# Seven-product matrix groups of a three-block transformer kernel: partial products chained in three PSUM pairs and added straight into the output quadrants

## The reference

```python
def sq_relu_mlp(h, w_up, w_down):          # twice: layers 0 and 1, D_FF = 4096
    return jnp.square(jax.nn.relu(h @ w_up)) @ w_down
...
    u = causal_depthwise_conv(h @ w_up[l].astype(h.dtype), ffn_conv_w[l], ffn_conv_b[l])
    u_val, u_gate = jnp.split(u, 2, axis=-1)   # width D_FF_2 = 2816 each
    x = x + (jax.nn.silu(u_gate) * u_val) @ w_down[l].astype(x.dtype)
```

## Time and profile before

| | |
|---|---|
| median of 3 runs | 1903.86 us (1903.72 to 1904.85) |
| span of the profiled execution | 1900.5 us |
| matmuls / DVE / ACT instructions | 9486 / 1988 / 1587 |
| DVE and ACT busy | 1339.4 and 985.3 us |

### The profile page before, as it was taken

How to read it: one execution, slowest core, us unless ns; L and a number is a source line. 1 busy time by engine, 2 the same in 40 slices (tenths; PEclk the granted TensorE clock), 3 DMA queues, 4 the chain that set the end, 5 groups by cost and what they waited for, 6 DMA issues and landing times. The chain is left out here.

```text
span 1900.5 us, 25399 instructions
## 1 busy us (share of the span) xinstructions
PE 1890.5 (99%) x9486; PEld 1555.8 (82%) x9486; DVE 1339.4 (70%) x1988; ACT 985.3 (52%) x1587; POOL 95.3 (5%) x114
## 2 busy tenths in 40 slices
PE   9999999999999999999999999999999999999999
PEld 8877888887888778888888988667788888888887
DVE  7656665656566766665566788998897867767867
ACT  5634464544546746454444435788445446545454
POOL 0100000101000000000100000000000000100101
PEclk9999999999999999999999999999999999999999
DMA  7632156757323114756752356222224634644735
GB/s 230 155 100 94 73 142 180 166 162 202 123 79 144 46 56 132 201 139 173 180 162 67 112 143 167 89 90 78 89 91 143 166 89 155 155 148 118 199 95 122
DMA packets 69676, 249.79 MB, mean 131 GB/s; under 512 B 7730, under 2 KB 7986, under 8 KB 68916
## 3 DMA queue, kind: packets, MB, share of 16 engines
q1 hardware_dynamic: 55728, 198.88, 31.0%
q0 software_dynamic: 13824, 49.29, 14.8%
q10 hardware_dynamic: 4, 0.00, 0.0%
HBM read 246.05 MB, written 2.10 MB: 131 GB/s over the span
## 5 line engine op out<-in xcount | busy, mean ns | idle before, releaser
L545 PE MATMUL ps<-HH,WH 128*128 128x512 f32 (+1 forms) x1696 | 626.2, 369 | 0.9 <-ACT AT L1736 0.9
L547 PE MATMUL ps<-HH,WL 128*128 128x512 f32 (+1 forms) x1696 | 621.2, 366 | 0.0
L546 PE MATMUL ps<-HL,WH 128*128 128x512 f32 (+1 forms) x1696 | 620.9, 366 | 0.0
L1299 ACT ACTIVATE WH<-WR 128x1024 fp32r<-128x1024 f32 x333 | 348.9, 1056 | 479.8 <-PE ps L547 315.3
L2030 DVE TENSOR_TENSOR WL<-WR,WH 128x1024 fp32r<-128x1024 f32 (+1 forms) x332 | 403.1, 1218 | 263.1 <-ACT WH L1299 262.4
L545 PEld LDWEIGHTS ps<-HH,WH 128*128 128x128 f32 x1696 | 319.9, 189 | 62.5 <-issue 11.6
L547 PEld LDWEIGHTS ps<-HH,WL 128*128 128x128 f32 x1696 | 319.9, 189 | 52.2
L546 PEld LDWEIGHTS ps<-HL,WH 128*128 128x128 f32 x1696 | 320.0, 189 | 50.7
L959 PE MATMUL ps<-WH,AH 128*128 128x512 f32 x490 | 191.0, 390 | 0.4 <-DVE WL L2030 0.4
L960 PE MATMUL ps<-WH,AL 128*128 128x512 f32 x490 | 190.7, 389 | 0.0
L961 PE MATMUL ps<-WL,AH 128*128 128x512 f32 x490 | 190.6, 389 | 0.0
(11 more groups left out here) (386 smaller groups left out, 2606.9 us busy)
## 6 DMA issues: line engine op xcount, KB each, us to landing
WR<-in_up SPq DMA_DIRECT2D x96, 512.0 KB, 4.2
WR<-in_quart SPq DMA_DIRECT2D x60, 512.0 KB, 3.6
WR<-in_quart POOLq DMA_DIRECT2D x48, 512.0 KB, 6.3
WR<-in_in SPq DMA_DIRECT2D x48, 512.0 KB, 3.6
WR<-in_down SPq DMA_DIRECT2D x16, 512.0 KB, 3.5
WR<-in_quartf SPq DMA_DIRECT2D x14, 512.0 KB, 3.5
WR<-in_quartf POOLq DMA_DIRECT2D x14, 512.0 KB, 5.6
MT<-in_up SPq DMA_DIRECT2D x12, 512.0 KB, 4.1
```

Of the source, the lines that this page charges most:

```text
L545: e.matmul(ps, wh, hi[:, c, cols], start=c == 0, stop=False)
L546: e.matmul(ps, wh, lo[:, c, cols], start=False, stop=False)
L547: y = e.matmul(ps, wl, hi[:, c, cols], start=False, stop=c == x.n - 1)
L1299: e.activation(x.wh[:, 0:n], raw(m, x.raw)[:, 0:n], AF.Copy).then_inc(*k.mark("whi", u))
```

## The change

The order of a group becomes b11, b21, t1 (half 0), b11, b21, t1 (half 1), then t2, b22, t3, t4. Seven products now use three pairs of banks: t2 goes on adding in the pair of b11, t3 goes on in that same pair, b22 goes on in the pair of t1, and t4 starts afresh in the pair of b21. Each time the pair has been taken out once before the next product continues in it, and PE waits for that. With the running sums, each `part` goes straight to the output quadrants: seven products make eight DVE operations a group, one each and two for t3. The accumulators PX and U2 and the `together` operations go. The first write to a quadrant is a copy, or a multiplication by -1 for t2. The groups of sevenf0 and sevenf1 do the same on X, and their POOL adds now go by `M_SUMS`. In `seven`, DVE now does the `part` that is due ahead of the cut of unit j+3. The last four down units wait for the last unit of the third group instead of `together`. Fewer matmuls start with an overwriting write; their number and shapes stay.

```diff
@@ -225,7 +225,7 @@
         add(f"up{layer}3", up[24:])
-        add(f"down{layer}3", down, extra=m.EXTRA["mlp"], freed=("sum7", layer, 6))
+        add(f"down{layer}3", down, extra=m.EXTRA["mlp"], freed=("unit", at[f"seven{layer}2"] + 13))
         if layer == 0:
@@ -315,13 +315,11 @@
     m.AL = arena("AL", [128, 4, 7, 256], 28, F32R)
-    m.PX = arena("PX", [128, 3, 2, 512], 59)
     m.H3H = arena("H3H", [128, DC, T], 0, F32R)
...
     m.SF = arena("SF", [128, 2, 4, 256], 56)
-    m.U2 = arena("U2", [128, 2, 512], 64)
@@ -385,13 +383,6 @@
-def partial(m, what):
-
-    if what in ("b21", "t2", "t3"):
-        return m.PX[:, ("b21", "t2", "t3").index(what)]
-    return quarter(m, *{"b11": (0, 0), "b22": (0, 1), "t4": (1, 0), "t1": (1, 1)}[what])
-
-
 def mixes(m, key):
@@ -473,7 +464,7 @@
 GLA_O = (6, 7)
-STREAM = [("b11", 0), ("b21", 0), ("t1", 0), ("b11", 1), ("b21", 1), ("t1", 1), ("b22", 0), ("b22", 1), ("t2", 0), ("t2", 1),
+STREAM = [("b11", 0), ("b21", 0), ("t1", 0), ("b11", 1), ("b21", 1), ("t1", 1), ("t2", 0), ("t2", 1), ("b22", 0), ("b22", 1),
           ("t3", 0), ("t3", 1), ("t4", 0), ("t4", 1)]
@@ -481,7 +472,7 @@
 M_SUMS = [("t1", 0), ("t1", 1), ("t2", 0), ("t2", 1), ("t3", 0), ("t3", 1), ("t4", 0), ("t4", 1)]
-F_SUMS = [("t1", 0), ("t1", 1), ("t2", 0), ("t3", 0), ("t3", 1), ("t2", 1), ("t4", 0), ("t4", 1)]
+LAST_SUMS = [("t1", 0), ("t1", 1), ("t2", 0), ("t3", 0), ("t3", 1), ("t2", 1), ("t4", 0), ("t4", 1)]
 LAST_BANKS = {"b11": 0, "b21": 2, "t1": 4, "b22": 6, "t2": 0, "t3": 0, "t4": 2}
@@ -495,9 +486,10 @@
 V_DECAYS, V_TURNS = (1, 4, 7, 10), (3, 6, 9, 12)
-SEVEN_BANKS = {"b11": 0, "b21": 2, "t1": 4, "b22": 6, "t2": 0, "t3": 2, "t4": 4}
-FFN_PARTS = {"b11": (((0, 0), 1), ("u2", 1)), "b21": (((0, 0), 1),), "t1": (((0, 1), 1), ((1, 1), 1)), "b22": (((0, 1), 1),),
-             "t2": (("u2", 1),), "t3": (((1, 0), 1), ((1, 1), -1)), "t4": (((1, 0), 1),)}
+SEVEN_BANKS = {"b11": 0, "b21": 2, "t1": 4, "b22": 4, "t2": 0, "t3": 0, "t4": 2}
+SEVEN_STARTS = ("b11", "b21", "t1", "t4")
+SEVEN_PARTS = {"b11": (((0, 0), 1),), "b21": (((0, 0), 1),), "t1": (((1, 1), 1),), "t2": (((0, 1), -1),), "b22": (((0, 1), 1),),
+               "t3": (((1, 1), -1), ((1, 0), 1)), "t4": (((1, 0), 1),)}
 GLA_DS = ((2, 3), (4, 5))
@@ -956,9 +948,9 @@
             e.wait_ge(*k.on("side", key, 4 * o + p, SIDE_PART[f]))
-            e.matmul(m.ps[b + v], xh, x.wh[:, w], start=start and q == 0, stop=False, skip_group_check=last)
-            e.matmul(m.ps[b + v], xl, x.wh[:, w], start=False, stop=False, skip_group_check=last)
-            y = e.matmul(m.ps[b + v], xh, x.wl[:, w], start=False, stop=stop and q == n - 1, skip_group_check=last)
+            e.matmul(m.ps[b + v], xh, x.wh[:, w], start=start and q == 0, stop=False, skip_group_check=True)
+            e.matmul(m.ps[b + v], xl, x.wh[:, w], start=False, stop=False, skip_group_check=True)
+            y = e.matmul(m.ps[b + v], xh, x.wl[:, w], start=False, stop=stop and q == n - 1, skip_group_check=True)
         return y
@@ -976,7 +968,7 @@
                 e.wait_ge(*k.on(*k.free[b + v]))
-            y = pairs(j, h, b, f, v, h == 0 and not (last and what in ("t2", "t3")), h == 1)
+            y = pairs(j, h, b, f, v, h == 0 and what in SEVEN_STARTS + ("b22",) * last, h == 1)
             if last and what == "t2" and h and v == 0:
@@ -2426,6 +2418,7 @@
     post, then = ("post_mlp0", "mix1") if layer == 0 else ("post_mlp1", "in2")
+    prior = {}
@@ -2442,22 +2435,27 @@
         u = at[f"seven{layer}{o}"] + STREAM.index((what, 1))
-        src, acc = pair(m, SEVEN_BANKS[what]).rearrange("p (a f) -> p a f", a=2), partial(m, what)
+        src = pair(m, SEVEN_BANKS[what]).rearrange("p (a f) -> p a f", a=2)
         e.wait_ge(*k.on("unit", u))
-        if o == 0:
-            e.tensor_copy(acc, src).then_inc(*k.mark("part", layer, o, what))
-        else:
-            e.wait_ge(*k.on("part", layer, o - 1, what))
-            e.tensor_tensor(acc, src, acc, A.add).then_inc(*k.mark("part", layer, o, what))
-
-    def together(n):
-
-        c11, c12, c21, c22 = (quarter(m, i, j) for i in range(2) for j in range(2))
-        p2, u2, u3 = (m.PX[:, i] for i in range(3))
-        out, a, b, op = ((u2, c11, u2, A.add), (c11, c11, p2, A.add), (u3, u2, u3, A.add), (c21, c21, u3, A.add),
-                         (c12, c12, c22, A.add), (c12, c12, u2, A.subtract), (c22, c22, u3, A.subtract))[n]
-        e.wait_ge(*(k.on("sum7", layer, n - 1) if n else k.on("part", layer, 2, "t4")))
-        e.tensor_tensor(out, a, b, op).then_inc(*k.mark("sum7", layer, n))
+        for to, sign in SEVEN_PARTS[what]:
+            acc = quarter(m, *to)
+            if to not in prior:
+                if layer == 0:
+                    e.wait_ge(*k.on("turned", "mlp0", 3, 1))
+                else:
+                    e.wait_ge(*k.on("turned", "mlp1", 3, 1))
+                if sign > 0:
+                    e.tensor_copy(acc, src).then_inc(*k.mark("part", layer, o, what, to))
+                else:
+                    e.tensor_scalar(acc, src, -1.0, None, A.mult).then_inc(*k.mark("part", layer, o, what, to))
+            else:
+                e.wait_ge(*k.on("part", *prior[to]))
+                if sign > 0:
+                    e.tensor_tensor(acc, src, acc, A.add).then_inc(*k.mark("part", layer, o, what, to))
+                else:
+                    e.tensor_tensor(acc, acc, src, A.subtract).then_inc(*k.mark("part", layer, o, what, to))
+            prior[to] = (layer, o, what, to)
+        k.also("part", layer, o, what)
@@ -2467,7 +2465,6 @@
                     plain(24 + j - 1)
-                    together(j - 1)
                 continue
@@ -2480,13 +2477,13 @@
         for j in range(14):
+            if j and STREAM[j - 1][1]:
+                part(o, STREAM[j - 1][0])
             v_cut(e, k, u + j + 3)
...
                 v_side_s(e, k, layer, 4 * o + 3)
-            if j and STREAM[j - 1][1]:
-                part(o, STREAM[j - 1][0])
         part(o, STREAM[13][0])
@@ -2896,8 +2893,6 @@
             v_cut(e, k, f_unit(k, j) + 4)
-            if a == 32 and n in (1, 3, 5):
-                together(n // 2)
             if n > 1 and n % 2 == 0:
@@ -2919,13 +2914,11 @@
             e.wait_ge(*k.on("unit", u))
-        for to, sign in (LAST_PARTS if o == 2 else FFN_PARTS)[what]:
-            acc = (m.U2[:, :, :] if to == "u2" else quarter_x(*to))[:, vs]
+        for to, sign in (LAST_PARTS if o == 2 else SEVEN_PARTS)[what]:
+            acc = quarter_x(*to)[:, vs]
             if to in prior:
                 e.wait_ge(*k.on("part", "f", *prior[to]))
-            if to == "u2" and not o and what == "b11":
-                e.tensor_copy(acc, src).then_inc(*k.mark("part", "f", o, what, to))
-            elif sign > 0:
+            if sign > 0:
                 e.tensor_tensor(acc, src, acc, A.add).then_inc(*k.mark("part", "f", o, what, to))
@@ -2934,19 +2927,14 @@
-    def together(n):
-
-        acc, op = ((quarter_x(0, 1), A.subtract), (quarter_x(1, 0), A.add), (quarter_x(1, 1), A.subtract))[n]
-        e.wait_ge(*k.on("part", "f", 1, "t4"))
-        e.tensor_tensor(acc, acc, m.U2[:, :, :], op).then_inc(*k.mark("part", "f", "u2", n))
-        prior[((0, 1), (1, 0), (1, 1))[n]] = ("u2", n)
-
     def seven(o):
...
                 break
+            if j and o < 2 and stream[j - 1][1]:
+                part(o, stream[j - 1][0])
             v_cut(e, k, u + j + 3)
@@ -2954,8 +2942,6 @@
                 v_side_s(e, k, "f", LAST_HIDDEN[o] // 2)
-            if j and o < 2 and stream[j - 1][1]:
-                part(o, stream[j - 1][0])
         if o < 2:
@@ -3013,7 +2999,7 @@
     u = k.at[name]
-    for what in F_SUMS if key == "f" else M_SUMS:
+    for what in LAST_SUMS if name == "sevenf2" else M_SUMS:
         j = stream_of(name).index(what)
```

## The result

The changed kernel takes 1953.35 us (median of 5, 1950.76 to 1954.81) beside 1903.72 us: the ratio is 1.0259, with a 95% interval of 1.0247 to 1.0271. It is slower by about 50 us. The forecast was 1937 with a range up to 1950: the direction and the place of the loss were right, the size was too small, and the range ended 3 us too low.

A forecast was written before the change was run, and what follows sets the result against it. PE, 99% busy, was taken as the bound. Waits of 17.6 us (four quiet groups), 14.1 (two with gain loads) and 1.3 (sevenf0, sevenf1) sum to 33.0 on 1900.5, plus 3.4 around the span: 1936.9 us; range 1914 to 1950.

The forecast's parts named there:

- DVE's saving: Fifteen fewer DVE operations at 1.22 us: 18 us off DVE, 0 off the end, since PE doesn't wait for them.
- The chain: Weight sums: b22 and t3 share a raw slot, so PE waits at unit 10, 4.4 us in each quiet group.
- Step 2: In seven00, unit 8's cut on DVE waits behind unit 7's cut and b21's part: begins at 287.7, done at 288.9 us.
- Step 3: In seven00, t3's load follows unit 8's cut, so t3's add goes out at 292.6 us, 6.3 us later.
- Step 4: In seven00, t2's part stands behind unit 10's cut and ends at 301.9; unit 10 is due at 297.5: 4.4 us wait.
- sevenf0 and sevenf1: Gated layer's two groups: t1's part slightly late for unit 8, 0.6 us each, 1.3 in all; bounds 0 and 3 each.
- the rival of the falling clock: Clock falls to 1.2 GHz for one unit after each of six waits, 2.7 us each: 1953 us; chance 0.09.
- a wait of 7.7 us each: In seven02 and seven12, t2's add takes 8.8 us beside the gain tile; 14.1 us together, less seven02's 1.3 of today.
- The section on the PSUM pairs: Continuing pairs have two units, 5.4 us, for a 1.22 us part: fits t2 and b22 in quiet groups; t3 depends on DVE.
- The prediction's own signs: Right: eleventh unit late, t3's add at 22 us, groups 42 to 46 us, DVE near 1321 us. Wrong: clock at 0.5.
- the rival with quicker transfers: Adds in the chain take 4.4 us once they run apart, so groups wait less: 1917 us; chance 0.14.
- PE's pace in the groups: Faster rival: without accumulator traffic the 0.227 us between matmuls falls; 11 ns less gains 14.8 us: 1889 us; chance 0.03.

The follow-up runs named there:

- e8_both: Changed kernel with own raw slots for t3, t1's half 1 earlier, t2's part ahead of unit 10's cut, bank ring from 4, later gain tiles: 1902.94 us, ratio 0.9993.
- e1_slots: Changed kernel with two raw slots of their own for t3's halves in the six groups of layers 0 and 1: 1910.02 us, ratio 1.0031.
- e6_order_dve: Kernel before with the new order of products and DVE's new order, but accumulators and four PSUM pairs kept (no chaining): 1940.81 us, ratio 1.0196.
- e2_warm: Changed kernel with 16 matmuls whose result nobody reads ahead of unit 10 in the six groups of layers 0 and 1: 1939.92 us, ratio 1.0189.
- e3_part: Changed kernel with DVE doing t2's part ahead of unit 10's cut in the six groups of layers 0 and 1: 1943.12 us, ratio 1.0205.
- e4_order: Kernel before with only t2 ahead of b22 in the groups' order and M_SUMS for sevenf0 and sevenf1: 1949.6 us, ratio 1.0242.
- e7_gain: Changed kernel with the two 1 MB gain tiles loaded only behind the up units after the third groups: 1945.64 us, ratio 1.0220.

## Why the prediction was right and wrong

**DVE's saving is hidden: right.** DVE's busy time fell by 16 us, the sum said 18, and e8_both shows that it is worth nothing measurable at the end (0.9984 to 1.0002).

**The chain: right step by step in seven00, and in sum with some luck.** t2's second add went out 8.4 us after the group's first matmul, as before. It took 5.3 us where I took 5.5:

```profile
DMA to landing us min/median/max: 5.3/5.3/5.3
```

Step 2 put unit 8's cut 17.3 us into the group, and it began at 288.16 - 271.09 = 17.1. Step 3 put t3's add at 22.2 us, and it went out at 293.26 - 271.09 = 22.2. Step 4 gave PE's restart at 31.5 us and it was 31.2; the stop was 4.0 us, not 4.4. The other three groups without a gain tile stopped for 4.8, 6.5 and 4.4 us, the two with one for 7.3 and 6.8, where I had 7.7. Together, less the 1.3 us of before, that is 32.4 us against the forecast's 31.7. The closeness is in part luck: the quiet groups stopped for 19.6 us where I had 17.6, and the other two added 12.8 where I had 14.1. e1_slots shows by removal that the shared slot is the cause, and e6_order_dve shows the same wait when the order is added without the chaining.

**sevenf0 and sevenf1: right.** 1.0 us together, against 1.3. The steps of the prediction gave a wait of 0.4 us each (1661.1 less 1660.7), and it took 0.6 without saying why; the stops were 0.3 and 0.5 us.

**What failed.** The step is the one that let each wait cost its own length: "a wait of 7.7 us each" and "4.4 us in each", summed with PE at full pace behind them. I had this as the rival of the falling clock, priced at 16 us, and gave it 0.09, because no row of before showed a stop that long. It happened in all six groups and cost 13.2 us. e2_warm, which fills the stops with work, gets 13.4 us back by the medians. With it the sum is 1950, and a wait that I overlooked adds 1.6: the twelve last up units begin at bank 2, which is now t4's, and its part is not done when sevenf1 ends. The section on the PSUM pairs looked at the groups alone and put nothing down for this:

```profile
1848.76 0.39 PE L953 MATMUL ps<-WL,AH 128*128 128x512 f32 x1
1850.55 0.47 PE L537 MATMUL ps<-HH,WH 128*128 128x512 f32 x1 [1.41 <-DVE X L2922]
```

That makes 1952, and 1953.35 was measured (1951.54 in the profiled execution). The 3.4 us that the prediction set around the span came from two different executions, and in each one on record it is 1.8 to 2.5 us; the sum adds to the median, so nothing hangs on it. The bounds had the same gap: I let the clock rival fall outside the range as one case in ten, though by the forecast itself stops of 4 to 8 us were the likely case, and the only question was what the clock does behind one. The prediction's own signs came out mixed: the late eleventh unit, t3's add 22 us into the group and DVE at 1323 us spoke for it, the granted clock at its lower level against it, and the groups lasted 43.8 to 48.1 us where it had 42 to 46.

**The other rivals.** The adds did not come down to the 4.4 us of the rival with quicker transfers: in the four groups without a gain tile t2's second add took 5.3 to 5.6 us and t3's 5.4 to 7.8. By the Trainium skill, page "DMA: Bandwidth & Descriptors", section "Anatomy of one DMA", the estimate was 3.2 us; the trace doesn't agree. PE's pace in the groups didn't change: 0.227 us from start to start wherever the clock is at its upper level.

## What to carry to other kernels

Where one engine is busy for 99% and waits for nobody, work taken from another is worth nothing, and an order that leaves a chain of slots and transfers less time can only cost: write down, for each unit that moves, which buffer its load takes and who must be done with it. When an operation has to stand in an engine's queue, put it ahead of what waits for a transfer, if its own input is ready first. And when a new wait of several microseconds is forecast on PE, price the clock behind it along with the wait.

## What the runs showed of the hardware

In the groups of seven of the changed kernel, e3_part, e4_order, e6_order_dve and e7_gain PE stopped for 2.3 us or more thirty times. Behind 29 of these stops the granted clock went to its lower level, for 6 to 14 matmuls of 128x512, which took 0.427 us from start to start instead of 0.227; the shortest such stop was 2.3 us. In five cases the first two to four matmuls behind the stop still ran at full pace. Behind one stop, of 3.35 us (e3_part, seven01), and behind all of up to 2.1 us the clock stayed up, so the length of a stop alone does not settle it. The Trainium skill, page "TensorE: Matmul & The Clock Gate", section "HAM oscillation", says that PE's idle stretches while it waits for a DMA bring the lower clock, and here the trace agrees in all but that one. In the changed kernel a stop of 4 to 6.7 us cost another 1.6 to 2.8 us. With sixteen matmuls whose result nobody reads ahead of the wait, the clock stayed up in five groups of six, in one of them behind 3.0 us of stop that were left, and the kernel took 13.4 us less.

An adding DMA of 512 KB (t2's second one in a group) took 5.3 to 5.6 us nearly alone in the changed kernel, 6.9 to 8.1 us when t3's plain loads of the same size ran beside it (e1_slots), and 7.9 to 10.8 us beside 1 MB of gains (the changed kernel and the one before). A plain load took 3.3 us in the kernel before and 3.6 us in the changed one, nearly alone.
